# Moving the activation buffers of a one-layer hybrid block by 192 bytes in SBUF

## The chip, the cores and the metric

The kernel runs on one core of a Trainium2 chip. The metric is the device time of one execution in microseconds (us), median of several runs. A profiled execution gives a trace: the start and duration of every instruction on TensorE (PE, with its weight loads as PEld), VectorE (DVE), ScalarE (ACT) and GpSimd (POOL), the DMA packets, and the clock that TensorE was granted.

## The reference

One encoder layer on a sequence of 256 tokens of width 2048, in float32:

```python
mod = silu(c) @ w_ada + b_ada                      # 2048 -> 6 x 2048
h = rms_norm(x) * (1 + sc_a) + sh_a
p = h @ w_in                                       # 2048 -> 3912
# three head groups: latent attention (low-rank q and kv), stick-breaking, forgetting
o = concat(head_rms_norm(o_mla), head_rms_norm(o_sb), head_rms_norm(o_fx))
x = x + g_a * (o @ w_out)                          # 2048 -> 2048
h = rms_norm(x) * (1 + sc_m) + sh_m
x = x + g_m * (square(relu(h @ w_ff1)) @ w_ff2)    # 2048 -> 8192 -> 2048
return rms_norm(x)
```

## The kernel before

**Three products for one.** Each float32 product is made from rounded parts. A weight tile is loaded into `raw`; ScalarE copies it to `w_hi` (type fp32r), and GpSimd (line 687, up to the output projection) or VectorE (line 757, in the two feed-forward products) writes the remainder `raw - w_hi` to `w_lo`. Activations are kept in the same way as a high and a low part, side by side: `hT` and `act` have the shape [128, tiles, 2, 256]. The product is then w_hi times the high part, w_hi times the low part, and w_lo times the high part.

**Units.** The weights come as 362 units of 512 KB, [128, 2, 512] each, through a ring of four slots (`RING`). A unit is 24 matmuls in the usual form (`unit`, lines 1165 to 1183): the weights are the stationary operand, 128 columns at a time, and the activations move, 256 columns; 16 matmuls at line 1175 with w_hi, 8 at line 1181 with w_lo. In the turned form (`turned_unit`, lines 1185 to 1200), used for the value blocks, the activations are stationary and the weights move, 512 columns: 8 matmuls at line 1193 and 4 at line 1198. Every matmul has its own weight load, so while one matmul streams its moving operand, the stationary operand of the next is read.

**Order.** The SP queue issues all loads, for the ring and for the 192 tiles of w_ada, in an order written out by hand. Stages: spreading c and the first norm; the input projection in 64 units (operand `hT`); the latent projections in 10 units (operand `lat`) interleaved with the attention heads; the output projection in 32 units (`oT`, then `hT`); the norm; then two halves of the feed-forward part, 64 units with `hT` and 64 with `act` in each; the last norm and the stores. VectorE also multiplies the w_ada tiles by c (line 776), whose partial sums go to `part_sum`, one column for each of 48 tiles.

Of the kernel before, what the change touches and what calls it, by code (L numbers as in the profile page):

```python
# [22 lines left out]
P = 128  # L23
D, S, FF = 2048, 256, 8192
EPS = 1e-6
KT = D // P
# [108 lines left out]
def hybrid_block(nc, xt_in, cols_in, consts_in, w_ada, weights, out):  # L135
    ctx = ExitStack()
    with ctx:
        def sb(name, shape, dt=F32, at=ctx):
            return at.enter_context(nc.sbuf_tensor(name, shape, dt))
# [16 lines left out]
        gain = sb("gain", [P, KT])  # L156
        plus_one = sb("plus_one", [P, 2 * KT])
        half_sum = sb("half_sum", [P, 2])
        part_sum = sb("part_sum", [P, 3 * KT])
        rstd = sb("rstd", [P, 2, S])  # L160
        small = sb("small", [P, KT])
        row = sb("row", [P, 2, HEADS])
# [1353 lines left out]
```

## Time and profile before

| | us |
|---|---|
| median of 3 runs | 1234.96 (1234.68 to 1239.51) |
| the profiled execution | 1234.67 |
| its span, first to last instruction | 1232.9 |

The span is what the rows of the trace add up to; 1.8 us of the profiled execution lie around it. A duration in the trace is the time in which one instruction is in flight. Matmuls overlap, so their rate is read from the starts: the start of one group of instructions to the start of the next, divided by the number of instructions in the first.

### The profile page before, as it was taken

The page shows a single profiled execution, that of the slowest core. Times are in us where ns is not written, and L with a number is a line of the kernel's source. Part 1 is how long each engine was busy: PE and PEld are TensorE (multiplying, and loading weights), DVE is VectorE, ACT ScalarE, POOL GpSimd, SP SyncE. Part 2 cuts the span into 40 slices and gives each one's busy share as a digit, 9 for nine tenths or more (in the row PEclk, how much of TensorE's full clock was granted, in tenths as well). Part 3 has the DMA queues.
Part 4 walks back from the last instruction along what each step waited for, and adds up shares of the span by engine and source line. Part 5 has one row for each costly group of instructions (what it writes and reads, how often), then busy time and mean ns, then how long its engine had stood idle before and what let it go on. Part 6 is the DMA issues. An engine that isn't in the chain of part 4 may idle for free.

```text
span 1232.9 us, 21623 instructions
## 1 busy us (share of the span) xinstructions
PE 1157.6 (94%) x9066; PEld 1122.5 (91%) x9066; DVE 746.2 (61%) x964; ACT 520.0 (42%) x627; POOL 295.6 (24%) x139
## 2 busy tenths in 40 slices
PE   4979999689988997999999999999999999999996
PEld 3879998678668997999999999999999999999995
DVE  5587568946976648767777444444455554455454
ACT  4533344336445445444444333333444444343341
POOL 2767887375306980000000000000000000000000
PEclk8999999889989998999999999999999999999998
DMA  9899899769863984887876555555555655555551
GB/s 343 312 390 374 341 351 400 290 239 336 298 208 103 360 328 186 305 272 258 292 273 193 186 184 186 182 181 186 184 175 188 187 173 190 187 181 180 186 171 69
DMA packets 81312, 296.87 MB, mean 241 GB/s; under 512 B 9025, under 2 KB 9153, under 8 KB 81217
## 3 DMA queue, kind: packets, MB, share of 16 engines
q1 hardware_dynamic: 81216, 295.50, 68.2%
q8 instruction: 72, 1.18, 0.4%
q14 instruction: 24, 0.19, 0.0%
HBM read 293.37 MB, written 2.10 MB: 240 GB/s over the span
## 4 chain that ended last, share of the span: by engine, by line
PE 78%; DMA 6%; DVE 6%; issue 4%; POOL 3%; ACT 2%; SPq 0%; DVEq 0%; ACTq 0%; POOLq 0%
PE ps L1175 47%; PE ps L1181 24%; DMA ada<-in_ada 4%; DMA raw<-in_weights 2%; POOL w_lo L687 2%; PE ps L1337 2%; DVE ada L776 1%; DVE o_tok L1078 1%; ACT w_hi L410 1%; PE ps L1193 1%; PE ps L1231 1%; DVE qk L842 0%; PE ps L1224 0%; PE ps L1347 0%; PE ps L1305 0%
## 5 line engine op out<-in xcount | busy, mean ns | idle before, releaser
L410 ACT ACTIVATE w_hi<-raw 128x1024 fp32r<-128x1024 f32 x362 | 382.0, 1059 | 555.6 <-PE ps L1181 448.4
L757 DVE TENSOR_TENSOR w_lo<-raw,w_hi 128x1024 fp32r<-128x1024 f32 x256 | 317.2, 1246 | 309.0 <-ACT w_hi L410 308.3
L1175 PE MATMUL ps<-hT,w_hi 128*128 128x256 f32 x3072 | 404.6, 285 | 26.4 <-DVE hT L883 13.2
L1175 PEld LDWEIGHTS ps<-hT,w_hi 128*128 128x128 f32 x3072 | 386.6, 194 | 29.3 <-issue 22.2
L687 POOL TENSOR_TENSOR w_lo<-raw,w_hi 128x1024 fp32r<-128x1024 f32 x106 | 255.1, 2425 | 117.2 <-ACT w_hi L410 116.9
L1175 PE MATMUL ps<-act,w_hi 128*128 128x256 f32 x2048 | 266.6, 283 | 0.0
L1175 PEld LDWEIGHTS ps<-act,w_hi 128*128 128x128 f32 x2048 | 255.0, 192 | 0.0
L1181 PE MATMUL ps<-hT,w_lo 128*128 128x256 f32 x1536 | 217.8, 285 | 0.0
L1181 PEld LDWEIGHTS ps<-hT,w_lo 128*128 128x128 f32 x1536 | 200.5, 194 | 0.0
L681 POOL TENSOR_TENSOR ssq<-ssq,sq 128x1024 f32<-128x1024 f32 x6 | 14.4, 2407 | 696.0 <-ACT sq L417 696.0
L1181 PE MATMUL ps<-act,w_lo 128*128 128x256 f32 x1024 | 143.7, 283 | 0.0
L1181 PEld LDWEIGHTS ps<-act,w_lo 128*128 128x128 f32 x1024 | 132.1, 192 | 0.0
L776 DVE CUSTOM_DVE_ANT_0 ada<-ada,ps,part_sum 128x1024 f32<-128x1024 f32 x48 | 60.1, 1276 | 24.8 <-DMA ada<-in_ada 24.3
L776 DVE CUSTOM_DVE_ANT_0 ada<-ada,ps,cols 128x1024 f32<-128x1024 f32 x48 | 60.5, 1278 | 12.5 <-DMA ada<-in_ada 11.4
L776 DVE CUSTOM_DVE_ANT_0 ada<-ada,ps,half_sum 128x1024 f32<-128x1024 f32 x32 | 40.8, 1280 | 16.0 <-DMA ada<-in_ada 14.1
L776 DVE CUSTOM_DVE_ANT_0 ada<-ada,ps,plus_one 128x1024 f32<-128x1024 f32 x32 | 40.4, 1277 | 11.8 <-DMA ada<-in_ada 7.3
L1193 PE MATMUL ps<-w_hi,hT 128*128 128x512 f32 x128 | 33.9, 409 | 8.6 <-DVEq L844 8.6
L1175 PE MATMUL ps<-oT,w_hi 128*128 128x256 f32 x256 | 35.2, 293 | 5.2 <-issue 5.2
L1175 PEld LDWEIGHTS ps<-oT,w_hi 128*128 128x128 f32 x256 | 33.3, 200 | 5.4 <-issue 5.4
L1193 PEld LDWEIGHTS ps<-w_hi,hT 128*128 128x128 f32 x128 | 24.4, 197 | 14.4 <-DVEq L844 9.6
L656 ACT ACTIVATE act<-tmp 128x1024 fp32r<-128x1024 f32 x16 | 16.9, 1058 | 34.0 <-DVE tmp L1123 34.0
L1129 DVE TENSOR_TENSOR act<-tmp,act 128x1024 fp32r<-128x1024 f32 x16 | 19.6, 1225 | 18.0 <-ACT act L656 18.0
(192 smaller groups left out, 758.1 us busy)
## 6 DMA issues: line engine op xcount, KB each, us to landing
raw<-in_weights SPq DMA_DIRECT2D x362, 512.0 KB, 4.2
ada<-in_ada SPq DMA_DIRECT2D x192, 512.0 KB, 5.9
xT<-in_xt SPq DMA_DIRECT2D x4, 512.0 KB, 7.0
y<-tmp SPq DMA_DIRECT2D x2, 512.0 KB, 2.6
consts<-in_consts SPq DMA_DIRECT2D x1, 580.0 KB, 6.9
y<-sq SPq DMA_DIRECT2D x1, 512.0 KB, 2.6
y<-ssq SPq DMA_DIRECT2D x1, 512.0 KB, 2.6
cols<-in_cols SPq DMA_DIRECT2D x1, 219.5 KB, 2.6
```

The costliest lines, as they stand in the source:

```text
L410: sc.activation(w_hi[:, slot, :, :], raw[:, slot, :, :], ACT.Copy).then_inc(hi_done, 1)
L656: sc.activation(act[:, 4 * b + 8 * it:4 * b + 8 * it + 4, 0, :], tmp2[:, :, :], ACT.Copy).then_inc(act_hi, 1)
L681: gp.tensor_tensor(ssq[:, :, :], ssq[:, :, :], sq[:, :, :], ALU.add).then_inc(ssq_done, 1)
L687: gp.tensor_tensor(w_lo[:, slot, :, :], raw[:, slot, :, :], w_hi[:, slot, :, :].bitcast(F32), ALU.subtract).then_inc(lo_pool, 1)
L757: ve.tensor_tensor(w_lo[:, slot, :, :], raw[:, slot, :, :], w_hi[:, slot, :, :].bitcast(F32), ALU.subtract).then_inc(lo_vec, 1)
L776: ve.tensor_tensor_reduce(out=ada[:, slot, :], in0=ada[:, slot, :], scale=1.0, scalar=part if second else bias, in1=c, op0=ALU.mult, op1=A ...
L1078: ins = ve.tensor_scalar(o, o, hss[:, q, AT_ML + n:AT_ML + n + 1], None, ALU.mult)
L1129: ve.tensor_tensor(act[:, 4 * it:4 * it + 4, 1, :], tmp2[:, :, :], act[:, 4 * it:4 * it + 4, 0, :].bitcast(F32), ALU.subtract).then_inc(ac ...
L1175: pe.matmul(acc[:, n, :], w, rhs[:, kt0 + k, half, :], start=first and k == 0 and n % 2 == 0 and half == 0, stop=False, skip_group_check=True)
L1181: ins = pe.matmul(acc[:, n, :], w_lo[:, slot, k, n * P:(n + 1) * P], rhs[:, kt0 + k, 0, :], start=False, stop=last and k == UK - 1, skip_g ...
L1193: pe.matmul(acc[:, t, :], lhs[:, kt0 + k, half, t * P:(t + 1) * P], w_hi[:, slot, k, :], start=first and k == 0 and half == 0, stop=False, ...
L1337: pe.matmul(s[:, q * P:(2 * q + 1) * P], lhs[:, q * P:(q + 1) * P], rhs[:, 0:(q + 1) * P], start=q == 0 and m == 0, stop=False, skip_group ...
```

## The change

`part_sum` gets 96 columns for 48. The new columns are not used. Everything allocated after it starts 192 bytes further on in its partition.

```diff
         plus_one = sb("plus_one", [P, 2 * KT])
         half_sum = sb("half_sum", [P, 2])
-        part_sum = sb("part_sum", [P, 3 * KT])
+        part_sum = sb("part_sum", [P, 6 * KT])
         rstd = sb("rstd", [P, 2, S])
         small = sb("small", [P, KT])
         row = sb("row", [P, 2, HEADS])
```

`hT`, `oT`, `act`, `pT`, `qk` and `consts` then lie 192 bytes modulo 256 past `w_hi` and `w_lo`, and `lat` and what lies beside it 224 bytes. `raw`, `w_hi`, `w_lo`, `xT`, `ada`, `c_rep`, `tmp`, `tmp2` and `cols` stay. No instruction, wait or transfer is added or taken away.

## Rows read from the trace of the kernel before

**Rows 1.** The page's busy time, and TensorE, its clock and DMA in 40 slices.

```profile
PE 1157.6 (94%) x9066; PEld 1122.5 (91%) x9066; DVE 746.2 (61%) x964; ACT 520.0 (42%) x627; POOL 295.6 (24%) x139
...
PE   4979999689988997999999999999999999999996
...
PEclk8999999889989998999999999999999999999998
DMA  9899899769863984887876555555555655555551
```

**Rows 2.** Stages by window: length, busy us and count by engine, granted clock, DMA share, GB/s.

```profile
64.00:228.00 164.00, 154.21 (x1115) 145.81 (x1114) 124.81 (x179) 68.27 (x77) 123.00 (x52) 0.99 0.95 366
228.00:360.00 132.00, 111.78 (x676) 90.09 (x676) 98.72 (x182) 64.66 (x146) 54.09 (x34) 0.93 0.77 279
...
400.00:466.00 66.00, 66.00 (x552) 66.00 (x551) 37.57 (x62) 27.29 (x26) 55.70 (x24) 1.00 0.91 339
482.65:660.00 177.35, 177.35 (x1480) 177.35 (x1479) 131.25 (x150) 80.41 (x82) 0.00 (x0) 1.00 0.76 262
660.00:1216.90 556.90, 556.90 (x4643) 556.90 (x4642) 270.82 (x241) 220.84 (x211) 7.23 (x3) 1.00 0.55 178
```

**Rows 3.** Waits in 482.65:1219: engine and line, for whom, us, times, longest.

```profile
ACT w_hi L410 <- PE ps L1181: 378.1, 219, 2.1
DVE w_lo L757 <- ACT w_hi L410: 304.4, 198, 2.1
```

**Rows 4.** TensorE's timeline, `hT` moving, feed-forward: start us, us in flight.

```profile
488.41 2.08 PE L1175 MATMUL ps<-hT,w_hi 128*128 128x256 f32 x16
490.33 1.12 PE L1181 MATMUL ps<-hT,w_lo 128*128 128x256 f32 x8
491.29 2.08 PE L1175 MATMUL ps<-hT,w_hi 128*128 128x256 f32 x16
```

**Rows 5.** The same with `act` moving, near the end.

```profile
1208.41 2.08 PE L1175 MATMUL ps<-act,w_hi 128*128 128x256 f32 x16
1210.33 1.12 PE L1181 MATMUL ps<-act,w_lo 128*128 128x256 f32 x8
1211.29 2.08 PE L1175 MATMUL ps<-act,w_hi 128*128 128x256 f32 x16
```

**Rows 6.** The same with `lat` moving.

```profile
271.64 1.09 PE L1181 MATMUL ps<-lat,w_lo 128*128 128x256 f32 x8
272.58 2.03 PE L1175 MATMUL ps<-lat,w_hi 128*128 128x256 f32 x16
274.44 1.09 PE L1181 MATMUL ps<-lat,w_lo 128*128 128x256 f32 x8
275.38 0.38 PE L1296 MATMUL ps<-sp,consts 128*128 128x256 f32 x1
```

**Rows 7.** The turned form with `hT` stationary.

```profile
115.58 1.98 PE L1193 MATMUL ps<-w_hi,hT 128*128 128x512 f32 x8
117.39 1.07 PE L1198 MATMUL ps<-w_lo,hT 128*128 128x512 f32 x4
118.30 0.28 PE L1175 MATMUL ps<-hT,w_hi 128*128 128x256 f32 x1
```

**Rows 8.** The turned form with `lat` stationary.

```profile
290.78 1.10 PE L1198 MATMUL ps<-w_lo,lat 128*128 128x512 f32 x4
291.72 0.59 PE L1296 MATMUL ps<-sp,consts 128*128 128x256 f32 x2
...
296.22 1.10 PE L1198 MATMUL ps<-w_lo,lat 128*128 128x512 f32 x4
297.15 0.38 PE L1296 MATMUL ps<-sp,consts 128*128 128x256 f32 x1
```

**Rows 9.** `lat` moving at the lower clock; then that window: PE busy, clock, DMA, GB/s.

```profile
260.91 1.91 PE L1175 MATMUL ps<-lat,w_hi 128*128 128x256 f32 x8
262.63 0.41 PE L1181 MATMUL ps<-lat,w_lo 128*128 128x256 f32 x1
...
260.91:262.63 1.72, 1.72 (x10) 0.50 0.43 105
```

**Rows 10.** One operation of each engine on both placements: ns min/median/max.

```profile
L883 DVE TENSOR_TENSOR hT<-tmp,hT x8: 689/694/1601, 29.4 to 181.0; 128x512 fp32r<-128x512 f32 x8
L820 DVE TENSOR_TENSOR lat<-tmp,lat x3: 684/687/693, 238.1 to 246.6; 128x512 fp32r<-128x512 f32 x3
L447 ACT ACTIVATE hT<-tmp x8: 630/632/636, 28.7 to 180.4; 128x512 fp32r<-128x512 f32 x8
L455 ACT ACTIVATE lat<-tmp x3: 630/631/634, 232.4 to 244.7; 128x512 fp32r<-128x512 f32 x3
```

## Prediction

> **What bounds the kernel now.** I read the page first. TensorE is in flight for 94% of the span, VectorE for 61%, and in the last two thirds of the slices TensorE shows nines while DMA falls to fives [rows 1]. The windows make this exact [rows 2]: from 482.65 to 1216.9 us, the feed-forward part, TensorE never stops, its clock is full, DMA moves 178 to 262 GB/s where it moves 366 GB/s in the early stage, and VectorE, the busiest of the others, is at 131.25 of 177.35 us, or 74%, in the part where it has w_ada tiles as well. The waits say who follows whom [rows 3]: ScalarE waits for TensorE to free a slot, VectorE waits for ScalarE, and TensorE does not appear as one that waits. In the early stage (64 to 228 us) DMA is at 0.95 and sets the pace; in the output projection (400 to 466 us) TensorE is without a gap and DMA is at 0.91, close behind.
>
> So about 60% of the kernel is a stream of matmuls whose rate alone sets the time. The timeline gives that rate. In the feed-forward part a unit of 24 matmuls takes 491.29 - 488.41 = 2.88 us with `hT` [rows 4], and 1211.29 - 1208.41 = 2.88 us with `act` [rows 5]: 120.0 ns a matmul. 256 units are 6144 matmuls, and 6144 x 120.0 ns = 737 us; the two windows have 6123 in 734.25 us, which agrees.
>
> **Is 120 ns what the streaming costs?** The lower clock says no. There 8 matmuls of 256 columns start in 262.63 - 260.91 = 1.72 us, 215 ns each, at a granted clock of 0.50 (1.2 GHz) [rows 9]. Halved, that is 107.5 ns at 2.4 GHz, an estimate. 12.5 ns of each 120 are thus something else, which shows at full clock only. The turned form loses the same: 12 matmuls in 118.30 - 115.58 = 2.72 us, 226.7 ns for 512 columns [rows 7], against 2 x 107.5 = 215, so 11.7 ns. Its columns are twice as many, but it has one weight load like the other. The loss goes with the weight load, not with the columns: two reads of SBUF that get in each other's way.
>
> Does it depend on where the operands lie? `lat` answers, as it lies 32 bytes past the weights. Moving, it takes (275.38 - 271.64) / 32 = 3.74 / 32 = 116.9 ns [rows 6], a loss of 9.4 ns, 3.1 less than when level. Stationary in the turned form it takes 0.94 / 4 = 235 ns once and 0.93 / 4 = 232.5 ns once [rows 8]; I take 234, a loss of 19 ns, 7.3 more than level in the same form. In that case the moving operand is 32 bytes short of the stationary one. So the trace has three places for moving against stationary: +32 loses 9.4 ns, level 12.5 ns (11.7 turned), -32 loses 19 ns. Placement counts, and it can go either way.
>
> **The change part by part.**
> 1. *The unused columns.* The line adds no instruction and no transfer; its cost is 0.
> 2. *ScalarE, VectorE and GpSimd on moved buffers.* The same subtraction takes 694 ns with `hT` and 687 ns with `lat`, the same copy 632 and 631 ns [rows 10]. I take 0. The bound is 7 ns for each of some hundred such operations, 1 us at most, which the waits hide [rows 3]. The w_lo and w_hi operations, which set the ring's pace, touch no moved buffer.
> 3. *Matmuls of the usual form on `hT`, `oT` and `act`.* The moving operand is 192 bytes past the stationary one. No row has this. Every step of 512 bytes (column tiles, slots, high and low part) leaves the rate as it is, since all 24 matmuls of a unit keep 120 ns [rows 4, 5]; so the pattern repeats after 512 bytes or after a part of it. If it repeats after 256, 192 past is 64 short, and the nearest row is the one at 32 short, 7.3 ns dearer than level; level is 64 away and +32 is 96 away. If it repeats after 512 only, +32 is the nearest, at 160 bytes, and tells little. The price is thus bounded by +7.3 ns from above and, below, by the whole loss going away, -12.5 ns. I lean to the side of the nearest row and take half of its surplus, as 192 lies beyond it and not on it: +3.65 ns, 123.65 ns a matmul.
>    Feed-forward: 6144 x 3.65 ns = 22.4 us, all of it on the path, since TensorE is the one that never waits. Output projection: some 570 x 3.65 ns = 2.1 us, likewise.
> 4. *The latent projections.* `lat` goes from +32 to 224 past, which is 32 short modulo 256. 192 matmuls, from 116.9 ns to between 116.9 and 127.3: 0 to 2 us, of which I take 1, as attention's chain and waits stand between them.
> 5. *The input projection.* 64 units with a DMA share of 0.95 [rows 2]. TensorE's 1115 matmuls there need 1115 x 120 = 134 of 164 us; at 127.3 ns they need 142. The cover is 22 us in sum, so I take 0 in both directions. If loads ceased to cover it, 1115 x 3.65 ns = 4 us would come on top.
> 6. *The turned form.* 192 matmuls on `hT` lie in that same stage: 0. After them, 24 on `lat` change by 0.3 us at most.
>
> Sum: 22.4 + 2.1 + 1 = 25.5 us on the profiled execution's 1234.67 us, which is 1260.2 us. The median of the runs, 1234.96, is 0.3 us away; I say 1260 us. Nothing else becomes late: a unit of 24 x 123.65 ns = 2.97 us gives ScalarE, VectorE and DMA more room than they have.
>
> A rule speaks against all of this. The Trainium skill ("SBUF — State Buffer", Who interferes with whom) has TensorE with two independent read ports, one for the moving operand and one for the weight load, and only the port pair of VectorE and GpSimd as a place of contention. By it the sum would be 0 and the time 1235 us. The trace does not agree: 120.0, 116.9 and 226.7 against 234 ns differ by placement alone.
>
> **The rivals.**
> - *Faster (the other side).* The matmul stream gets the +32 rate or better. Mechanism: being level is itself what makes the two reads meet, and any shift away from it lets them pass. For it: +32 is 3.1 ns cheaper than level. Against: -32 is a shift too, and dearer. Price at the +32 rate: 6714 x 3.1 ns = 21 us, so 1214 us. If the whole loss goes: 6144 x 12.5 = 77 us, and in the output projection DMA at 0.91 stops the gain at 0.09 x 66 = 6 us, so 1152 us. VectorE would not stop it before: 74% of a 2.88 us unit is 2.13 us and the unit would be 2.58 us. It decides as soon as the pitch is under 119 ns.
> - *No change.* 192 bytes are three quarters of the period or a whole number of a shorter one, and the two reads meet as they do when level; or the loss has another cause than the relative place. For it: the rate is exactly 120.0 ns through 250 units, as of something that locks. Against: the `lat` rows. Time 1235 us.
> - *Slower by the full surplus of the row at 32 short.* 6144 x 7.3 = 45 us, 570 x 7.3 = 4 us, and 2 us in `lat`: 1286 us.
>
> **How the numbers follow.** Half a per cent, 6 us, is about what a measurement of this kernel tells from no change; it is 0.9 ns a matmul. Slower has 0.45: the period of 256 with its nearest row speaks for it, but that period is not shown. Faster has 0.37: some 0.2 around 1214 us, the rest between 1205 and 1152 us. No change has 0.18. The predicted time is that of the slower case, 1260 us, whose own range is 1242 to 1286. The range for 8 in 10 runs from 1182 us, which cuts off about 0.12 of the large gains, to 1288 us, which leaves 0.07 for losses above the dearest row.
>
> **What the profile after would show.** In the feed-forward windows the unit of 24 matmuls would take 2.97 us for 2.88, equal in `hT` and `act`, with TensorE still without a gap; at the lower clock the rate would stay 215 ns; VectorE's and ScalarE's durations would stay. The early stage would keep its length to within 2 us. `lat` moving would go from 116.9 towards 127 ns. The prediction is wrong if the unit takes 2.86 us or less, or if the pitch stays at 120.0 ns; it is wrong in its reason if the time is gained or lost in a place where no moved buffer feeds a matmul.

## The result: 1196 us for 1235, and the profile after

The changed kernel took 1196.14 us (median, 1194.14 to 1198.26, 4 executions) against 1235.01 us: ratio 0.967, interval 0.966 to 0.969. The forecast was 1260 us, slower. The way it went was among the rivals ("Faster"), and 1196 us lies inside the stated range of 1182 to 1288 us.

The page of the changed kernel: busy time, and in 40 slices TensorE, its clock and DMA, to set beside [rows 1].

```profile
span 1192.4 us, 21623 instructions
...
PE 1111.2 (93%) x9066; PEld 1074.8 (90%) x9066; DVE 746.5 (63%) x964; ACT 519.6 (44%) x627; POOL 294.9 (25%) x139
...
PE   4979998769998897999999999999999999999995
...
PEclk8999999889998999999999999999999999999998
DMA  8899999759874599578887666665565666665651
```

The counts are the same. VectorE, ScalarE and GpSimd are busy for as long as before (746.2, 520.0 and 295.6 us there), and TensorE for 46 us less. The windows of the changed kernel, columns as in [rows 2], say where:

```profile
64.00:228.00 164.00, 150.26 (x1110) 140.50 (x1108) 126.16 (x179) 67.81 (x77) 123.42 (x53) 0.99 0.96 370
...
400.00:466.00 66.00, 66.00 (x562) 66.00 (x562) 39.53 (x65) 27.65 (x27) 56.91 (x25) 1.00 0.89 338
482.65:660.00 177.35, 177.35 (x1567) 177.35 (x1566) 138.62 (x158) 84.81 (x88) 0.00 (x0) 1.00 0.79 273
```

From 482.65 to 660 us TensorE does 1567 matmuls where it did 1480. The timeline of TensorE, with `hT` and with `act`, answers to [rows 4, 5]:

```profile
485.63 1.98 PE L1175 MATMUL ps<-hT,w_hi 128*128 128x256 f32 x16
487.45 1.07 PE L1181 MATMUL ps<-hT,w_lo 128*128 128x256 f32 x8
488.35 1.98 PE L1175 MATMUL ps<-hT,w_hi 128*128 128x256 f32 x16
...
1160.19 1.98 PE L1175 MATMUL ps<-act,w_hi 128*128 128x256 f32 x16
1162.01 1.07 PE L1181 MATMUL ps<-act,w_lo 128*128 128x256 f32 x8
1162.91 1.98 PE L1175 MATMUL ps<-act,w_hi 128*128 128x256 f32 x16
```

A unit of 24 takes 488.35 - 485.63 = 2.72 us for 2.88, with both operands: 113.3 ns a matmul for 120.0. The first feed-forward matmul starts at 477.96 us (before: 477.40) and the first matmul behind the last product, at line 1214, at 1176.52 us (before: 1217.05):

```profile
477.96 3.75 PE L1175 MATMUL ps<-hT,w_hi 128*128 128x256 f32 x16 [5.74 <-issue]
481.51 0.84 PE L1181 MATMUL ps<-hT,w_lo 128*128 128x256 f32 x3
...
1176.52 1.89 PE L1214 MATMUL ps<-ssq,cols 128*128 128x256 f32 x8
```

The same places in the kernel before:

```profile
477.40 3.76 PE L1175 MATMUL ps<-hT,w_hi 128*128 128x256 f32 x16 [5.75 <-issue]
480.96 1.87 PE L1181 MATMUL ps<-hT,w_lo 128*128 128x256 f32 x8
482.66 0.28 PE L1175 MATMUL ps<-hT,w_hi 128*128 128x256 f32 x1
...
1217.05 1.89 PE L1214 MATMUL ps<-ssq,cols 128*128 128x256 f32 x8
```

That is 698.56 us for 739.65, 41.1 us less, and 6144 x 6.67 ns = 41.0 us. The whole gain is there; the part of the kernel before it takes 0.6 us more. The first rows also show the lower clock (0.50 granted), with a start after a pause: 16 matmuls in 481.51 - 477.96 = 3.55 us, as before the change (480.96 - 477.40 = 3.56 us). At that clock the move changes nothing.

The output projection is different. Its units in the changed kernel:

```profile
401.22 2.05 PE L1175 MATMUL ps<-hT,w_hi 128*128 128x256 f32 x16
403.11 1.10 PE L1181 MATMUL ps<-hT,w_lo 128*128 128x256 f32 x8
404.05 2.05 PE L1175 MATMUL ps<-hT,w_hi 128*128 128x256 f32 x16
```

404.05 - 401.22 = 2.83 us, 117.9 ns: `hT` again, at the same distance and the same clock, and another rate. So at 192 bytes there are two rates. Which one an execution has in its feed-forward part is not fixed either, as the experiments show; the four executions of the result all had the lower time.

### The profile page after: what moved, and what is told of

Its sections match the earlier page's. It is cut to its first block, busy times and chain, and to the rows that moved or that the text cites. A ratio compares the mean times of both kernels' runs of the same rounds, so it can differ in the third digit from the quotient of the medians.

```text
span 1192.4 us, 21623 instructions
## 1 busy us (share of the span) xinstructions
PE 1111.2 (93%) x9066; PEld 1074.8 (90%) x9066; DVE 746.5 (63%) x964; ACT 519.6 (44%) x627; POOL 294.9 (25%) x139
## 4 chain that ended last, share of the span: by engine, by line
PE 70%; DMA 10%; POOL 7%; DVE 6%; issue 5%; ACT 2%; SPq 0%; DVEq 0%; ACTq 0%; POOLq 0%
PE ps L1175 42%; PE ps L1181 21%; POOL w_lo L687 6%; DMA raw<-in_weights 5%; DMA ada<-in_ada 4%; PE ps L1337 2%; DVE ada L776 2%; ACT w_hi L410 1%; DVE o_tok L1078 1%; PE ps L1231 1%; DVE qk L842 0%; PE ps L1224 0%; PE ps L1347 0%; POOL ssq L681 0%; PE ps L1217 0%
## 5 line engine op out<-in xcount | busy, mean ns | idle before, releaser
L1175 PE MATMUL ps<-hT,w_hi 128*128 128x256 f32 x3072 | 386.8, 279 | 26.8 <-DVE hT L883 13.3
L1175 PEld LDWEIGHTS ps<-hT,w_hi 128*128 128x128 f32 x3072 | 369.0, 190 | 30.3 <-issue 22.2
L1175 PE MATMUL ps<-act,w_hi 128*128 128x256 f32 x2048 | 252.9, 276 | 0.0
L1175 PEld LDWEIGHTS ps<-act,w_hi 128*128 128x128 f32 x2048 | 241.6, 188 | 0.0
L1181 PE MATMUL ps<-hT,w_lo 128*128 128x256 f32 x1536 | 209.0, 279 | 0.2 <-POOL w_lo L687 0.2
L1181 PEld LDWEIGHTS ps<-hT,w_lo 128*128 128x128 f32 x1536 | 191.7, 190 | 0.7 <-POOL w_lo L687 0.6
L1181 PE MATMUL ps<-act,w_lo 128*128 128x256 f32 x1024 | 136.9, 276 | 0.0
L1181 PEld LDWEIGHTS ps<-act,w_lo 128*128 128x128 f32 x1024 | 125.6, 188 | 0.0
```

The source lines that it names most:

```text
L1175: pe.matmul(acc[:, n, :], w, rhs[:, kt0 + k, half, :], start=first and k == 0 and n % 2 == 0 and half == 0, stop=False, skip_group_check=True)
L1181: ins = pe.matmul(acc[:, n, :], w_lo[:, slot, k, n * P:(n + 1) * P], rhs[:, kt0 + k, 0, :], start=False, stop=last and k == UK - 1, skip_g ...
```

## The experiments

Theory A is that the distance between the operand that moves and the one that is being loaded decides, and nothing else. Its rivals are that the place of the activations decides by itself (B), or that the gain is outside the matmul stream (C). In what follows, "rate" is the time from one matmul's start to the next in the feed-forward part, so a lower rate is a faster stream. It is read from one window of each profile, 660 to 1160 us, in which TensorE never stops: 500 us by the number of matmuls less the two in flight at its edge. These rows, of the kernel before and of the changed one, show the reading; the columns are the window, its length, TensorE's busy time and count, clock, DMA share and GB/s.

```profile
660.00:1160.00 500.00, 500.00 (x4169) 1.00 0.57 183
```

```profile
660.00:1160.00 500.00, 500.00 (x4414) 1.00 0.61 194
```

500 / 4167 = 120.0 ns before, 500 / 4412 = 113.3 ns after. A count of 4247, as in e4 below, is 500 / 4245 = 117.8 ns. A ratio is against executions of the kernel before that were taken along with that run.

**e1: everything moved, the distance kept.**

```diff
+        pad0 = sb("pad0", [P, 48])
         raw = sb("raw", [P, RING, UK, BW])
```

> An unused buffer of 192 bytes stands ahead of raw, so that all buffers move by 192 bytes and hT, oT and act stay level with w_hi and w_lo. Theory A (the distance between the moving and the stationary operand modulo 256 decides): 120.0 ns a matmul in the feed-forward part, about 1235 us. Theory B (the place of the activation buffers by itself decides, wherever the weights lie): 113.3 ns, about 1196 us. Theory C (the gain is outside the matmul stream): the unit of 24 stays at 2.88 us and the time falls all the same.

1236.55 us, ratio 1.000 (0.999 to 1.002), rate 120.0 ns (4169 in the window). Moving the activations does nothing if the weights go with them: B falls. C had fallen with the unit of 2.72 us, as the gain is in the stream.

**e2: the weights moved, the distance made.**

```diff
         raw = sb("raw", [P, RING, UK, BW])
+        pad0 = sb("pad0", [P, 16])
         w_hi = sb("w_hi", [P, RING, UK, BW], F32R)
         w_lo = sb("w_lo", [P, RING, UK, BW], F32R)
+        pad1 = sb("pad1", [P, 48])
```

> w_hi and w_lo are moved by 64 bytes and everything behind them by 256, so that the activations keep their place modulo 256 and still lie 192 bytes modulo 256 past the weights. Theory A: 113.3 ns a matmul in the feed-forward part, about 1196 us. Theory B: 120.0 ns, about 1235 us.

1197.89 us, ratio 0.969 (0.966 to 0.971), rate 113.3 ns (4414). The gain is there with the activations where they were modulo 256. Of the three only A is left, but for its "nothing else": at one distance there are two rates, so something besides the distance takes part. Here the output projection too has the lower rate:

```profile
403.94 1.98 PE L1177 MATMUL ps<-hT,w_hi 128*128 128x256 f32 x16
405.75 0.50 PE L1183 MATMUL ps<-hT,w_lo 128*128 128x256 f32 x3
```

405.75 - 403.94 = 1.81 us for 16, 113.1 ns.

**e3 and e4: the period.** `part_sum` 256 and 448 bytes longer.

```diff
-        part_sum = sb("part_sum", [P, 3 * KT])
+        part_sum = sb("part_sum", [P, 3 * KT + 64])     # e4: + 112
```

> Activation buffers moved by 256 bytes instead of 192. If the pattern repeats after 256 bytes: 120.0 ns a matmul and about 1235 us. If it repeats only after 512 (or it is enough not to start level): another rate than 120.0 ns, by 2 ns or more, and a time 12 us or more away from 1235 us.

> Activation buffers moved by 448 bytes, which is 192 modulo 256. Period of 256: 113.3 ns a matmul and 1196 us. Period of 512: 448 is 64 short and not 192 past, so another rate than 113.3 ns, by 2 ns or more.

e3: 1236.27 us, ratio 0.999 (0.998 to 1.001), 120.0 ns. The period is 256 bytes or a part of it (a part is ruled out by 128 bytes, below, which has another rate than level). e4 took 1221.1, 1222.96, 1197.41 and 1198.78 us; the one with a profile, 1221.1, has 117.8 ns. Two executions fell in each of two groups 24 us apart, and 6144 x (117.8 - 113.3) ns = 28 us is the distance that a full swap of the rates would give. The profile settles only that 448 bytes can give 117.8 ns; with the times it says that the two rates of the changed kernel are there at 448 too, as a period of 256 wants it.

**e5 to e10: the other distances.** The same line with 16, 32, 40, 56, 8 and 24 columns more.

> Activation buffers moved by 64 bytes. Theory D (the reads lock into one of a few rhythms, and the distance chooses which there are): 120.0, 117.8 or 113.3 ns a matmul through the whole feed-forward part, so 1235, 1222 or 1197 us. Theory E (the loss falls smoothly from 12.5 ns when level to 5.8 ns at 192): a rate between those, steady or not, near 118 ns.

> Activation buffers moved by 128 bytes, the farthest from level if the period is 256. Theory D: one of 120.0, 117.8 and 113.3 ns. Theory E (the farther from level the less loss): less than 113.3 ns, under 1196 us. Theory F (the loss is a matter of the 32-byte step and not of the distance): as at +32, near 117 ns, 1217 us.

> Activation buffers moved by 160 bytes. Theory D: 120.0, 117.8 or 113.3 ns. Theory E: between the rates at 128 and at 192. Theory F: near 117 ns.

> Activation buffers moved by 224 bytes, so that the moving operand is 32 short of the stationary one in the usual form, the place from which the forecast took its price. If the turned form's loss there carries over to the usual form: 127 ns a matmul and 1286 us. If it does not, as lat in the changed kernel has it: near 118 ns and 1224 us.

> Activation buffers moved by 32 bytes: hT and act where lat was in the kernel before. If lat's rate of 116.9 ns there was not bound to its short bursts: 6144 x 3.1 ns = 19 us and 2 us more in the output projection, 1215 us. If long streams lock: 120.0, 117.8 or 113.3 ns.

> Activation buffers moved by 96 bytes. Theory D (a few rhythms): a rate between 117.5 and 120 ns or 113.3 ns, 1197 or 1220 to 1235 us. Theory E (smooth): between 117.8 ns (at 64) and 118.7 ns (at 128), about 1226 us.

| bytes past the weights | matmuls in the window | rate, ns | median us (range, executions) | ratio (interval) |
|---|---|---|---|---|
| 0 (before) | 4169 | 120.0 | 1235.01 (1234.68 to 1239.51, 4) | 1 |
| 32 (e9) | 4289 | 116.6 | 1223.15 (1211.23 to 1226.64, 3) | 0.987 (0.978 to 0.996) |
| 64 (e5) | 4248 | 117.8 | 1223.76 (1221.53 to 1228.38, 3) | 0.989 (0.985 to 0.994) |
| 96 (e10) | 4169 | 120.0 | 1237.08 (1234.73 to 1239.82, 9) | 1.000 (0.999 to 1.002) |
| 128 (e6) | 4216 | 118.7 | 1229.26 (1225.68 to 1236.58, 9) | 0.994 (0.992 to 0.996) |
| 160 (e7) | 4216 | 118.7 | 1221.51 (1216.33 to 1225.40, 3) | 0.987 (0.981 to 0.992) |
| 192 (after) | 4414 | 113.3 | 1196.14 (1194.14 to 1198.26, 4) | 0.967 (0.966 to 0.969) |
| 224 (e8) | 4227 | 118.3 | 1228.77 (1225.25 to 1231.09, 5) | 0.992 (0.989 to 0.995) |

Theory E, a smooth curve, falls: 96 is as dear as level and 192 lies alone, 5 ns below both its neighbours. Theory D is right in part. The streams do repeat a fixed pattern: the starts in the trace are an even 120 ns apart when level, but at 96 bytes 117, 125, 116, 123, 118 and 121 ns in turn, which also makes 120.0 ns in the mean, and at 32 bytes 113, 116, 117 and 120 ns. But 116.6, 118.3 and 118.7 ns are none of its three rates. Theory F, near 117 ns at every distance that is not level, falls with 118.7 and 120.0 ns. At 32 bytes there are two rates in one profile: 116.6 ns in the feed-forward part, and 117.8 ns over the 192 matmuls with `oT` in the output projection. The execution with the profile took 1211.23 us and the other two 1223 and 1227 us. At 160 bytes the range of 9 us is no wider than that of the kernel before (1234 to 1243 us in one series), and tells nothing. e8 is the place from which the forecast took its price, and in the usual form it costs nothing more than level: 118.3 ns for the 127.3 that the turned form's loss would give.

**e11: only `hT` at 192, the rest level.**

```diff
-        part_sum = sb("part_sum", [P, 3 * KT])
+        part_sum = sb("part_sum", [P, 6 * KT])
         hT = sb("hT", [P, KT, 2, S], F32R)
+        pad1 = sb("pad1", [P, 16])
```

> Only hT lies 192 bytes modulo 256 past the weights; oT, act and the rest are moved by 256 bytes and stay level. Theory A: the first feed-forward product (3072 matmuls with hT) at 113.3 or 117.8 ns, the second (3072 with act) at 120.0 ns, so half of the gain: 3072 x 6.7 = 21 us, 1214 us, or 7 us, 1228 us. If the distance of something else did it: all or nothing, 1196 or 1235 us.

1217.95 us (1213.29 to 1219.65, 3 executions), ratio 0.985 (0.979 to 0.990). Three windows of its profile, the first and the third with `hT` moving, in the two halves of the feed-forward part, and the second with `act`:

```profile
500.00:640.00 140.00, 140.00 (x1192) 1.00 0.82 285
680.00:820.00 140.00, 140.00 (x1169) 1.00 0.57 184
860.00:1000.00 140.00, 140.00 (x1238) 1.00 0.62 193
```

That is 140 / 1190 = 117.6 ns with `hT` (unit by unit 117.8), 140 / 1167 = 120.0 ns with `act`, and 140 / 1236 = 113.3 ns with `hT` again. Each part changes with its own buffer. The stream with `hT` had the higher of the two rates of 192 bytes in the first half and the lower one in the second, after a stretch with `act` in between: the choice is made anew when the stream comes back to that distance.

**e14: only `w_lo` moved.** The matmuls of one unit then have two distances to the weights that are being loaded.

```diff
+        pad0 = sb("pad0", [P, 16])
         w_lo = sb("w_lo", [P, RING, UK, BW], F32R)
+        pad1 = sb("pad1", [P, 48])
```

> Only w_lo is moved, by 64 bytes, and what lies behind it by 256 in all: the activations are level with w_hi and 192 bytes modulo 256 past w_lo. If each matmul's rate depends on the distance to the weights being loaded meanwhile: the 16 matmuls with w_hi near 120.0 ns, the 8 with w_lo nearer 113.3 ns, 2048 x 6.7 = 14 us in sum, 1222 us. If the pace is set by one distance for the whole stream: 1235 or 1196 us.

1234.18 us, ratio 0.998 (0.997 to 1.000), 4198 in the window, 119.2 ns. A unit in its timeline:

```profile
701.03 2.08 PE L1177 MATMUL ps<-act,w_hi 128*128 128x256 f32 x16
702.95 1.11 PE L1183 MATMUL ps<-act,w_lo 128*128 128x256 f32 x8
703.89 2.08 PE L1177 MATMUL ps<-act,w_hi 128*128 128x256 f32 x16
```

The 16 with w_hi take 1.92 us (120.0 ns), the 8 with w_lo 0.94 us (117.5 ns), in turn through the whole part. So the rate changes from matmul to matmul with the place of the weights. It came out at the higher of the two rates of 192 bytes, not at 113.3 ns, which makes 2048 x 2.5 ns = 5 us for the 14 expected; the medians show 2 us. No one distance sets the pace of the whole stream.

**e15 and e16: steps finer than 32 bytes.** `hT` and `act` start 16 bytes into their buffers. Shown is the edit at `hT`; the one at `act` is like it, and `part_sum` has 40 (e15) or 48 (e16) columns more than before.

```diff
+        hT = sb("hT", [P, KT * 2 * S + 4], F32R)[:, 4:4 + KT * 2 * S].rearrange("p (k h s) -> p k h s", k=KT, h=2)
+        pad1 = sb("pad1", [P, 56])
```

> hT and act start 176 bytes past the weights (oT at 160). If only the 32-byte place matters, as at 160: 118.7 ns, 1228 us. If 16-byte steps matter: another rate; below 113.3 ns and 1196 us if the loss has its least there.

> hT and act start 208 bytes past the weights (oT at 192). If only the 32-byte place matters, as at 192: 113.3 or 117.8 ns, 1196 or 1223 us. If 16-byte steps matter: another rate.

e15: 1233.32 us, ratio 0.997 (0.996 to 0.999), 4195, 119.2 ns. e16: 1231.03 us (1212.88 to 1232.19, 4 executions), 4199, 119.1 ns. So steps of 16 bytes matter: the two profiled executions, 16 bytes to either side of 192, have lost most of the gain. One execution of e16 took 1212.88 us, without a profile, so 208 bytes may have a lower rate too. Nothing here beats 192.

**e13: the changed kernel again, six executions.**

> The changed kernel once more, for more executions. If the feed-forward part always falls into 113.3 ns: all executions between 1193 and 1200 us. If it was luck: some near 1196 + 6144 x 4.4 ns = 1223 us, as with 448 bytes.

1222.44, 1195.96, 1199.57, 1199.93, 1225.61 and 1221.16 us: it was luck in part. The profile is of the first, 4247 matmuls in the window, 117.8 ns:

```profile
700.68 1.11 PE L1181 MATMUL ps<-act,w_lo 128*128 128x256 f32 x8
701.63 2.05 PE L1175 MATMUL ps<-act,w_hi 128*128 128x256 f32 x16
```

701.63 - 700.68 = 0.95 us for 8. In the same execution it is the output projection that has the lower rate:

```profile
442.35 1.98 PE L1175 MATMUL ps<-oT,w_hi 128*128 128x256 f32 x16
444.16 1.07 PE L1181 MATMUL ps<-oT,w_lo 128*128 128x256 f32 x8
445.07 1.18 PE L1175 MATMUL ps<-oT,w_hi 128*128 128x256 f32 x9
```

445.07 - 442.35 = 2.72 us a unit, 113.3 ns. Of ten executions of the changed kernel seven took 1194 to 1200 us and three 1221 to 1226 us. Their median is 1199 us and their mean 1205 us. The clock does not part them: its mean is 0.966 to 0.976 in the seven and 0.968 to 0.975 in the three.

**e12, e17 and e18: what chooses between the two rates.** One extra matmul of n columns, ones times ones, goes into a PSUM bank that nobody uses, after a product of the feed-forward part.

```diff
                     (turned_unit if turned else unit)(u0 + j, split(use), rhs, kt0 + UK * j, ready(j), j == 0,
                                                       j == units - 1)
+                if u0 >= B_FF:                          # e18: if u0 == B_FF
+                    pe.matmul(ps[0][:, 2, 0:n], ones, cols[:, C_ONE:C_ONE + n], start=True, stop=True)
```

> The changed kernel with one extra small matmul (ones times ones, 64 columns, into a PSUM bank that nobody uses) after each of the 24 products of the feed-forward part. If the two rates at 192 bytes (113.3 and 117.8 ns) are rhythms that the stream falls into when it starts, and keeps: each product has one of the two from its start to its end, and they differ from product to product; with n of 24 products in the slower one the time is 1196 + 5 us for the extra matmuls + n x 1.1 us. If the slower rate comes from what runs beside the matmuls (the transfers of the output projection), all 24 products stay at 113.3 ns: 1201 us.

e12 (n = 64, after each of the 24 products): 1228.18 us (1223.55 to 1231.88, 9 executions). The first break in its timeline:

```profile
502.32 1.07 PE L1181 MATMUL ps<-hT,w_lo 128*128 128x256 f32 x8
503.23 0.33 PE L1209 MATMUL ps<-cols 128*128 128x64 f32 x2
503.37 2.13 PE L1175 MATMUL ps<-hT,w_hi 128*128 128x256 f32 x16
505.33 1.10 PE L1181 MATMUL ps<-hT,w_lo 128*128 128x256 f32 x8
506.28 0.99 PE L1175 MATMUL ps<-hT,w_hi 128*128 128x256 f32 x7
```

8 matmuls in 0.91 us ahead of it, 0.95 us behind it; the 23 products after it all stay at 117.8 ns, each break leading back to the same rate. The changed kernel has the same products without the breaks, and in its first profile they all ran at 113.3 ns. Here the rate changes at the break itself, so it is not made by what runs beside the stream; the stream falls into a rhythm after a break and keeps it.

> As e12, but the extra matmul after product i of the 24 in the feed-forward part has 4, 8, 12, ... 96 columns. If the choice between 113.3 and 117.8 ns hangs on the phase between the two reads at the start of a stream: some sizes put it into the one and some into the other, with a pattern in the size. If any break leads to 117.8 ns: 113.3 ns at most until the first extra matmul and 117.8 ns after all 23 that are followed by a product.

e17 (n = 4, 8, ... 96): 1220.95 us (2 executions). The product ahead of the first break was at 113.3 ns. The breaks of 4, 8, 12, ... 36 columns changed the rate each time, nine times in a row, so that 8, 16, 24 and 32 led to 113.3 ns and the others to 117.8. 40 to 80 left it at 117.8 (eleven), 84 led to 113.3, 88 back to 117.8, 92 left it there. One of each kind:

```profile
613.60 0.29 PE L1212 MATMUL ps<-cols 128*128 128x24 f32 x2
...
615.66 1.07 PE L1183 MATMUL ps<-hT,w_lo 128*128 128x256 f32 x8
616.56 0.62 PE L1177 MATMUL ps<-hT,w_hi 128*128 128x256 f32 x4
...
635.61 0.30 PE L1212 MATMUL ps<-cols 128*128 128x28 f32 x2
...
637.71 1.10 PE L1183 MATMUL ps<-hT,w_lo 128*128 128x256 f32 x8
638.65 1.58 PE L1177 MATMUL ps<-hT,w_hi 128*128 128x256 f32 x12
```

After 24 columns the groups of 8 go to 0.90 us, after 28 to 0.94 us. I read this as "sizes 8 to 32 in steps of 8 lead to the lower rate" and put one of 16 where it should help:

> The changed kernel with a single extra matmul of 16 columns after the first of the 24 feed-forward products. If that size leads to 113.3 ns from either rate: all executions between 1193 and 1201 us, none near 1223 us; against 3 of 10 slow ones without it, so many executions without a slow one would be a 3 in 100 event by luck with ten. If it only swaps the two rates, or its effect hangs on the phase in which it comes: a mixture of 1197 and 1223 us as before.

e18: 1223.38, 1220.88, 1197.47, 1224.76, 1220.48 and 1221.11 us. In its profile the extra matmul comes at 504.51 us into a stream at 113.3 ns and leaves it at 117.8:

```profile
503.61 1.07 PE L1181 MATMUL ps<-hT,w_lo 128*128 128x256 f32 x8
504.51 0.29 PE L1209 MATMUL ps<-cols 128*128 128x16 f32 x2
...
506.62 1.10 PE L1181 MATMUL ps<-hT,w_lo 128*128 128x256 f32 x8
507.56 0.64 PE L1175 MATMUL ps<-hT,w_hi 128*128 128x256 f32 x4
```

It swaps the rates and does not choose one: 16 columns led from 117.8 to 113.3 ns in e17 and from 113.3 to 117.8 ns here. Seven of ten executions of the changed kernel had the lower rate; after a swap most should be slow, and five of six were. The sixth, 1197.47 us, has no profile. The alternation in e17 was nine swaps. A break that leads to 113.3 ns from both rates was not found; of 84 columns, which led there from 117.8, it wasn't tried from 113.3.

## Why the prediction was wrong

- **What bounds the kernel** was right. The feed-forward part gave all of the gain, 41.1 us, of a span that is 40.5 us shorter, with TensorE without a gap and nobody else late.
- **That 120 ns holds a loss, tied to the weight load and to where the operands lie,** was right, and e1, e2, e11 and e14 show it: the distance between the two operands changes the rate, matmul by matmul within a unit (e14), though at 192 bytes it leaves two rates open. That it is the two reads of SBUF that meet is an inference from this; no run sees the reads themselves. The estimate of 12.5 ns for the whole loss is a little low, since the first two starts in the group of [rows 9] are 218 and 215 ns apart and the others 213. In the rows of the kernel before, above, 8 matmuls at the lower clock go from 480.96 to 482.66 us, 212.5 ns each; half of that is 106.3 ns, so the loss would be nearer 14 ns, of which 7 are left at 113.3 ns, an estimate. The rule of the Trainium skill ("SBUF — State Buffer", Who interferes with whom) that TensorE's two read ports are independent, by which the prediction has no change of time, does not describe this stream: 120.0 and 113.3 ns differ by the distance.
- **Step 3 of the change, "take half of its surplus", failed, in its sign.** It forecast +3.65 ns a matmul, or 22.4 us more in the feed-forward part; the profile of the result has -6.67 ns, or 41.1 us less. Two things in it were wrong. It carried the turned form's loss at 32 short over to the usual form: e8 measures that place at 118.3 ns, not 127.3. And it took a neighbour's rate for a guide: 160 and 224 bytes are at 118.7 and 118.3 ns and 192, between them, is at 113.3, and even 176 and 208 are at 119 in their profiles. With the period shown as 256, the nearest row would still have been the wrong one. The bounds, from -12.5 to +7.3 ns, held.
- **The turned form's 19 ns** were not a matter of the side either. In the changed kernel the moving weights are 32 bytes past `lat` and no longer 32 short, and four matmuls take 296.47 - 295.54 = 0.93 us, 232.5 ns, as in [rows 8]:

```profile
295.54 1.09 PE L1198 MATMUL ps<-w_lo,lat 128*128 128x512 f32 x4
296.47 0.59 PE L1296 MATMUL ps<-sp,consts 128*128 128x256 f32 x2
```

With `lat` level (e8) the same four take 296.44 - 295.53 = 0.91 us, 227.5 ns, so in this form both sides of level are dearer. With `hT` stationary the move made this form dearer: a turned unit goes from 114.47 to 117.27 us, 2.80 us or 233.3 ns a matmul, for 226.7 in [rows 7]. The weights are then 64 bytes past `hT`, a distance at which the usual form is cheaper than level. So one form's price by distance says nothing of the other's. The time does not show it, as that stage goes by DMA.
- **The rival "Faster"** had the right sign, but not the right reason. Its mechanism was that being level makes the reads meet and any shift helps; 96 bytes is a shift and costs 120.0 ns. "Locks" in the rival "No change" was nearer to it: the stream does lock, but into different rates at different distances.
- **The output projection** moved from 69.18 to 67.93 us of matmuls and started 1.4 us later, so it gave nothing; the forecast had a term of +2.1 us there.
- **The early stages** were covered as said: the feed-forward part starts 0.6 us later than before, with a DMA share of 0.96 in the stage that it bounds. The cover was smaller than step 5 has it: 144 of the 1115 matmuls are of the turned form, so they need about 149 us of the 164 and not 134. The median of VectorE's subtraction on `hT` went from 694 to 791 ns over 8 instructions, which is not the move: it is 976 ns in e1 and 785 ns in e3, both level, and 722 ns in e13.
- **`lat`** went from 116.9 ns (32 past) to 2.84 us a unit, 118.3 ns (224 past), for "towards 127":

```profile
271.84 2.06 PE L1175 MATMUL ps<-lat,w_hi 128*128 128x256 f32 x16
273.73 1.11 PE L1181 MATMUL ps<-lat,w_lo 128*128 128x256 f32 x8
274.68 0.59 PE L1296 MATMUL ps<-sp,consts 128*128 128x256 f32 x2
```

That it is 118 and not 127 says by itself that the turned form's price did not carry over.

What stays open is why 192 bytes have a rate that their neighbours lack, and what in the start of a stream picks one of two.

## What to carry to other kernels

Where matmuls follow each other without a gap and each has its own weight load, read the time of one matmul from the starts, compare it with half of its time at the lower clock, and if it is above, try the distance between the two operands in steps of 32 bytes; it costs one line and here was worth 3.3%, or 2.4% in the mean of ten executions. Try them all instead of reasoning from a neighbour. And look at the single times: a median of four showed one of two rates.

## What the runs showed that was not expected

- The rate of a gapless stream depends on the distance of its operands modulo 256 bytes, and not smoothly: 120.0, 116.6 or 117.8, 117.8, 120.0, 118.7, 118.7, 113.3 or 117.8, 118.3 ns in steps of 32.
- At one distance there can be two rates, at 192 bytes 113.3 and 117.8 ns. One holds for hundreds of microseconds, and one small matmul (0.14 us from its start to the next) can change it for the rest of the kernel.
- At the lower clock the same stream shows no dependence on these two distances: 16 matmuls in 3.56 us level and in 3.55 us at 192 bytes.
